# Seven-product block scheme in both feed-forward stages of a two-layer encoder kernel, with the Hyena filters moved between the output products

## The chip, the cores and the metric

The kernel runs on one core of one Trainium2 chip. The metric is the device time of one execution in microseconds (us). Engine names: PE is the matmul engine (TensorE), DVE VectorE, ACT ScalarE, POOL GpSimd, SP SyncE, which issues most DMAs. SBUF is the on-chip memory, PSUM the eight accumulator banks that PE writes.

## What is computed

768 tokens (512 of a prompt, 256 of a sample) of width 1024 pass two layers. Each layer is a half feed-forward step, a mixing part (RWKV-7 heads, neighbourhood attention, Hyena long convolution) and a second half feed-forward step. The reference, cut to what the change touches:

```python
def swiglu(x, w_in, w_out):
    gate, up = jnp.split(x @ w_in, 2, axis=-1)          # w_in 1024 x 5632, w_out 2816 x 1024
    return (jax.nn.silu(gate) * up) @ w_out

def encoder_layer(x, lp):
    x = x + 0.5 * swiglu(rms_norm(x, lp['norm_ffn1']), lp['ffn1_w_in'], lp['ffn1_w_out'])
    h = rms_norm(x, lp['norm_mix'])
    ...                                                  # mixing part, ends with x = x + mixed @ w_out
    return x + 0.5 * swiglu(rms_norm(x, lp['norm_ffn2']), lp['ffn2_w_in'], lp['ffn2_w_out'])

def hyena_filters(seq_len, lp):                          # 256 channels, two orders, two segments
    ...                                                  # z: 33 position features
    h = jnp.sin(freq * (z @ lp['hy_ff_w1'] + lp['hy_ff_b1']))
    h = jnp.sin(freq * (h @ lp['hy_ff_w2'] + lp['hy_ff_b2']))
    h = (h @ lp['hy_ff_w3']).reshape(seq_len, 2, HY_ORDER, C_DIM)
    h = h * jnp.exp(-t * jnp.abs(deltas))[:, None, None, :]
    ...                                                  # forward and flipped backward taps, joined to kern
    return kern / jnp.sum(jnp.abs(kern), axis=0, keepdims=True)   # its spectrum is used by the mixer
```

## The kernel before

**Data.** x lies transposed in SBUF, features on partitions: 8 tiles of 128 features x 768 tokens. Every main product is made of three matmuls (mm3, L898): each operand is split into a high part in fp32r and a low part, the rest, and high x high, high x low and low x high are added in PSUM. ACT makes the high part (a cast), DVE the low part (a subtraction). The token axis is cut into halves of 384 columns, so almost all matmuls have 384.

**Weights.** They come from memory in tiles of 1024 x 128 through wring, three buffers filled by SP in order of use (load_tile, L732). A buffer is refilled when DVE has made the low part of what it held (released, L719). The splits go to the rings wh and wl, 4 slots or 8 half slots.

**First feed-forward stage** (ffn, PE L987, ACT L1671, DVE L2209). 22 tiles of 128 gate features and as many of up features, in blocks of 6, 6, 5 and 5. For each tile j and token half PE makes gate and up: 2 x 8 x 3 = 48 matmuls, so 96 for a tile. ACT and DVE make the gated activation from them and split it. After a block the output part follows: 8 output tiles, two halves each, 3 matmuls for each of the block's tiles; DVE adds each result to x (add_out, L2146, who waits for PE there). Banks 0 to 3 belong to the input part, 4 to 7 to the output part. Behind the gate/up products stand the Hyena filter jobs, at the places named by FILTER_AT (a place is one token half of one tile): mlp (the two small layers), taps (the third layer, windowed by DVE, magnitudes taken by ACT, added up by POOL), sum (their total over partitions) and kern (the kernel's spectrum, by products with a table). They use banks 4 to 6.

**Second feed-forward stage** (ffn_pairs, PE L1050, ACT L1725, DVE L2315). Features are seen as 2 halves of 4 tiles, tokens as 2 halves, and [gate up] as 2 columns: a 2x2 block product made of seven products instead of eight. For a pair j of gate and up tile each product is 4 x 3 = 12 matmuls (product, L1036), 84 for the pair. A product i needs item i of the weights (a half tile of wring, or a sum that DVE makes in wsum at L2248, L2249 and L2257; split at L2267) and combination i of x (made once before the stage by pair_first and pair_second, L2373 and L2384, from x, gain and y1). Exits from PSUM: first_gate (L2276, L2277), second_up (L2284, L2286), second_gate (L2293, L2294), first_up, then gate_up twice and act_low1 twice; some products are held meanwhile by an ACT copy (hold, L1704). Blocks are 5, 5, 4, 4, 4. The ring has eight half slots: while pair j is multiplied, the items of pair j+1 are made (ahead), seven ahead. Output parts are as in the first stage.

**What sets the order.** Each engine runs its own program in the order written, and waits on semaphores. The combinations for the second stage are made while PE runs the last product of the mixing part (mix_out), whose tiles take 8 x 2 x 3 matmuls, in the order 0, 4, 1, 5, ... that completes pairs of tiles. The norm's sum of squares (add_squares, L2107) is joined to PE by norm (L904); its root (rstd) is not needed before the exits, since it scales columns.

## Time and profile before

| what | value |
|---|---|
| runs, device time | 3453.22, 3447.7, 3457.7 us; median 3453.22 |
| the profiled execution | 3456.03 us, of which the span of the engines 3454.2 |
| mean granted PE clock | 0.988 of full speed |
| PE, weight loads, DVE, ACT, POOL busy | 96%, 90%, 61%, 33%, 1% of the span |
| chain that ended last | PE 88%, DVE 8% |
| main matmuls with hh/hl (first stage and projections) | 3 x 2112, mean 340, 336 and 335 ns |
| main matmuls with the output activation | 3 x 1408, mean 335 ns |
| seven-product matmuls (L1033) | 3 x 1232, mean 336, 335 and 335 ns |

Matmuls overlap in the pipeline, so the duration of one is about twice the distance from one start to the next; costs are taken from distances. The order of stages in layer 0: first feed-forward stage from 28 to 617 us, projections and mixing to 1214, second feed-forward stage to 1730; layer 1 repeats this.

### The profile page before, as it was taken

To read this page: it belongs to the slowest core of one execution; us is meant where nothing else is said; L and a number is where in the kernel's file an instruction comes from. 1 tells how busy PE (TensorE), PEld (TensorE's weight loads), DVE (VectorE), ACT (ScalarE), POOL (GpSimd) and SP (SyncE) were. 2 spreads that over 40 slices of the span, in tenths; PEclk is the share of its full clock that TensorE was granted. 3 is DMA by queue.
4 is the path that set the end of the run, shared out by engine and by line. 5 is a ranking of instruction groups with operands and counts; after the bars stand their busy time and mean duration, and the time that the engine had idled before them with its cause. 6 is when DMAs were issued, how large, how long until landed. Compare 5 with 4: busy or idle time off the path is not lost.

```text
span 3454.2 us, 61563 instructions
## 1 busy us (share of the span) xinstructions
PE 3322.5 (96%) x26092; PEld 3125.4 (90%) x26092; DVE 2113.3 (61%) x3792; ACT 1153.1 (33%) x2015; POOL 50.4 (1%) x62
## 2 busy tenths in 40 slices
PE   7999999999998999999999999999999979999998
PEld 7999999888776899999999999998887768999997
DVE  5443444663878686666754534456548886776666
ACT  4221213221445353333431212132224544443333
POOL 0000000000000000000000000000000000000000
PEclk9999999999999999999999999999999999999999
DMA  3122121222033222222222121222310512222221
GB/s 136 61 78 69 61 74 56 104 96 85 4 115 137 68 62 73 72 68 68 69 77 80 63 84 48 73 88 78 106 59 5 197 54 80 65 69 72 71 68 67
DMA packets 80770, 264.36 MB, mean 77 GB/s; under 512 B 8994, under 2 KB 8994, under 8 KB 79216
## 3 DMA queue, kind: packets, MB, share of 16 engines
q1 hardware_dynamic: 76944, 248.08, 21.9%
q0 software_dynamic: 3552, 12.34, 1.1%
q8 instruction: 207, 3.39, 0.4%
q14 instruction: 67, 0.55, 0.1%
HBM read 230.50 MB, written 29.88 MB: 75 GB/s over the span
## 4 chain that ended last, share of the span: by engine, by line
PE 88%; DVE 8%; issue 2%; DMA 1%; ACT 1%; SPq 0%; DVEq 0%; ACTq 0%
PE ps L896 70%; PE ps L1033 18%; DMA gtab<-hyc 1%; DVE rstd L2107 0%; DVE uv L2735 0%; DVE sc L2785 0%; DMA bias<-bias 0%; DMA x<-xT 0%; PE ps L1489 0%; DVE M2X L2508 0%; ACT mh L2024 0%; DVE wl L2267 0%; DVE Mrk L2495 0%; DVE hout L2893 0%; DVE ktok L2496 0%
## 5 line engine op out<-in xcount | busy, mean ns | idle before, releaser
L896 PE MATMUL ps<-hh,wh 128*128 128x384 f32 (+2 forms) x2112 | 717.3, 340 | 11.5 <-DVE hl L2115 10.4
L896 PE MATMUL ps<-hl,wh 128*128 128x384 f32 (+2 forms) x2112 | 708.8, 336 | 0.0
L896 PE MATMUL ps<-hh,wl 128*128 128x384 f32 (+2 forms) x2112 | 708.4, 335 | 0.0
L896 PE MATMUL ps<-act_high,wh 128*128 128x384 f32 x1408 | 471.3, 335 | 1.7 <-DVE act_low L2313 1.7
L896 PE MATMUL ps<-act_high,wl 128*128 128x384 f32 x1408 | 470.4, 334 | 0.0
L896 PE MATMUL ps<-act_low,wh 128*128 128x384 f32 x1408 | 470.4, 334 | 0.0
L1624 ACT CAST wh<-wring 128x1024 fp32r<-128x1024 f32 (+3 forms) x300 | 261.7, 888 | 573.9 <-PE ps L896 541.6
L896 PEld LDWEIGHTS ps<-hh,wh 128*128 128x128 f32 x2112 | 398.8, 189 | 35.3 <-issue 16.0
L1033 PE MATMUL ps<-gh,wh 128*128 128x384 f32 x1232 | 414.1, 336 | 12.6 <-DVE gated L2284 4.3
L2146 DVE SCALAR_TENSOR_TENSOR x<-ps,x 128x384 f32<-128x384 f32 x320 | 177.4, 556 | 391.1 <-PE ps L896 390.9
L1033 PE MATMUL ps<-gh,wl 128*128 128x384 f32 x1232 | 412.9, 335 | 0.0
L1033 PE MATMUL ps<-gl,wh 128*128 128x384 f32 x1232 | 412.7, 335 | 0.0
L896 PEld LDWEIGHTS ps<-hl,wh 128*128 128x128 f32 x2112 | 399.1, 189 | 15.0 <-issue 0.3
L896 PEld LDWEIGHTS ps<-hh,wl 128*128 128x128 f32 x2112 | 398.7, 189 | 14.1
L2097 DVE TENSOR_TENSOR wl<-wring,wh 128x1024 fp32r<-128x1024 f32 (+3 forms) x300 | 304.2, 1027 | 67.6 <-ACT wh L1624 65.7
L896 PEld LDWEIGHTS ps<-act_high,wh 128*128 128x128 f32 x1408 | 264.3, 188 | 4.2 <-DVE act_low L2313 3.7
L896 PEld LDWEIGHTS ps<-act_low,wh 128*128 128x128 f32 x1408 | 264.3, 188 | 0.0
L896 PEld LDWEIGHTS ps<-act_high,wl 128*128 128x128 f32 x1408 | 264.3, 188 | 0.0
L1033 PEld LDWEIGHTS ps<-gh,wh 128*128 128x128 f32 x1232 | 232.4, 189 | 16.9 <-DVE gated L2284 5.0
L2221 DVE TENSOR_TENSOR silu<-ps,rstd 128x384 f32<-128x384 f32 x88 | 48.9, 556 | 323.3 <-PE ps L896 323.3
L1033 PEld LDWEIGHTS ps<-gl,wh 128*128 128x128 f32 x1232 | 232.4, 189 | 0.0
L1033 PEld LDWEIGHTS ps<-gh,wl 128*128 128x128 f32 x1232 | 232.1, 188 | 0.0
(305 smaller groups left out, 4642.1 us busy)
## 6 DMA issues: line engine op xcount, KB each, us to landing
wring<-wa SPq DMA_DIRECT2D x244, 512.0 KB, 3.5
wring<-wa SPq DMA_DIRECT2D x64, 320.0 KB, 2.8
wring<-wa SPq DMA_DIRECT2D x32, 384.0 KB, 3.1
bias<-bias SPq DMA_DIRECT2D x24, 512.0 KB, 8.3
wring<-wa SPq DMA_DIRECT2D x48, 256.0 KB, 2.5
conv_q_k<-stage SPq DMA_DIRECT2D x28, 384.0 KB, 2.6
kern_rows<-kst POOLq DMA_DIRECT2D x12, 512.0 KB, 3.3
outT<-x SPq DMA_DIRECT2D x2, 3072.0 KB, 10.3
```

Source lines behind the costliest of these rows:

```text
L896: return pe.matmul(out, lhsT, rhs, start=start, stop=stop)
L1033: m = pe.matmul(out, lhs[a], rhs[b], start=start and n == 0, stop=stop and n == 2, skip_group_check=onto)
L1624: sa.copy(wh[:, slot_of(t), 0:k, :], wring[:, t % RAWS, 0:k, :]).then_inc(s_whi, 1)
L2097: TT(wl[:, slot_of(t), 0:k, :], wring[:, t % RAWS, 0:k, :], wh[:, slot_of(t), 0:k, :].bitcast(F32), SU)\
L2146: STT(xs, bank(banks + v % 4, HALF), factor, xs, M, AD).then_inc(s_xup, 1)
L2221: TT(silu[:, u % 2, :], bank(2 * (u % 2), HALF), rstd[:, cols], M).then_inc(s_gate, 1)
```

## The change

Both feed-forward stages use ffn_pairs, and the ffn of three engines is gone. Six parts:

1. The first stage makes 84 matmuls for a pair in place of 96. Its combinations of x are made by start() in layer 0, and in layer 1 while PE runs the last output part of layer 0, whose tiles come in the order 0, 4, 1, 5, ... (pair_done with g = 2l + 2).
2. Blocks are 3, 3, 4, 4, 4, 4 in both stages.
3. The weight ring has 4 half slots (RING), and items, output tiles of the feed-forward part among them, are made three ahead (LEAD). The other half of the old ring's space holds filter buffers.
4. Filter jobs stand behind the output products of the first stage, at most to place 13 of the 16 of a block, and use banks 0 to 3.
5. They run in two halves of 128 channels: twice the jobs (24 of taps and kern in place of 12, 8 sums in place of 4), half the columns. hwt and dec hold one half at a time, and there is one table buffer.
6. x is loaded in pairs of tiles i and i + 4, and the kernels are stored by halves, in pieces of 128 columns.

The places of the filter jobs, block by block: block 0 has mlp at 0 and 4, taps at 9 and 10, sum 13; block 1 kern 0 and 4, taps 5 and 6, sum 9, kern 10; block 2 kern 0, taps 1, sum 4, kern 5, taps 6, sum 9, kern 10 (place 42 of the stage), taps 11 and 12 (places 43 and 44, the first of the second half); blocks 3 and 4 go on in the same way.

```diff
-FF_BLOCKS = [[(0, 6), (6, 6), (12, 5), (17, 5)], [(0, 5), (5, 5), (10, 4), (14, 4), (18, 4)]]
-FF_MOST = [max(n for _, n in b) for b in FF_BLOCKS]
-FF_OUTS = [2 * OUT_TILES * len(b) for b in FF_BLOCKS]
-FF_USES = [2 * FT + len(b) * OUT_TILES for b in FF_BLOCKS]
+FF_BLOCKS = [(0, 3), (3, 3), (6, 4), (10, 4), (14, 4), (18, 4)]
+FF_MOST = max(n for _, n in FF_BLOCKS)
+FF_OUTS = 2 * OUT_TILES * len(FF_BLOCKS)
+FF_USES = 2 * FT + len(FF_BLOCKS) * OUT_TILES
...
-UNITS = 7
-HALVES = 2 * SPLITS
+UNITS, RING, LEAD = 7, 4, 3
...
+FF_ITEMS = [t for b, (j0, nj) in enumerate(FF_BLOCKS)
+            for t in [("unit", j, i) for j in range(j0, j0 + nj) for i in range(UNITS)] + [("out", b, m) for m in range(OUT_TILES)]]
+ITEM_OF = {t: q for q, t in enumerate(FF_ITEMS)}
+ITEM_BASE = (2, 0)
...
-FILTER_AT = {2: ("mlp", 1), 5: ("mlp", 2), 7: ("taps", 0, 0, 0), 8: ("taps", 0, 0, 2), 9: ("sum", 0, 0),
-             13: ("kern", 0, 0), 14: ("kern", 0, 1), 15: ("taps", 1, 0, 0), 16: ("taps", 1, 0, 2), 18: ("sum", 1, 0),
-             20: ("kern", 1, 0), 21: ("kern", 1, 1), 25: ("taps", 0, 1, 4), 27: ("sum", 0, 1), 29: ("kern", 0, 2),
-             35: ("taps", 1, 1, 4), 37: ("sum", 1, 1), 39: ("kern", 1, 2)}
...
+CHH = C_DIM // 2
+TAP_GROUPS = [(h, o, s) for h in range(2) for s in range(2) for o in range(2)]
+KERN_ORDER = {(0, 0): (0, 1), (1, 0): (1, 0), (0, 1): (2,), (1, 1): (2,)}
...
+    jobs = [(0, ("mlp", 1)), (4, ("mlp", 2)), (4, None)]
+    for h, o, s in TAP_GROUPS:
+        jobs += [(1, ("taps", h, o, s, p)) for p in TAP_TILES[s][::2]] + [(3, ("sum", h, o, s))]
+        jobs += [(4 if n else 1, ("kern", h, o, a)) for n, a in enumerate(KERN_ORDER[o, s])]
+    out, at = {}, 0
+    for gap, job in jobs:
+        at += gap
+        if at % 16 > 13:
+            at = at // 16 * 16 + 16
...
+        def item_free(l, f, q):
+
+            if q >= RING:
+                return item_used(l, f, q - RING)
+            if f:
+                return s_fo, x_count(l, 2) + 2 * (4 + ring_place(f, q) // 2) + 2
...
+                for n, (h, o, s) in enumerate(TAP_GROUPS):
+                    add_magnitudes(l, n)
+                    p_last = TAP_TILES[s][-1]
+                    if o == 1 and (h, s) != (1, 1):
+                        pool.wait_ge(*fv.at(l, "win", h, o, p_last))
+                        load_decay(h + s, 1 - s)
+                    for a in KERN_ORDER[o, s]:
+                        pool.wait_ge(*fp.at(l, "kern", h, o, a))
+                        after = {(0, 0): 1, (1, 1): 0, (1, 0): 2, (1, 2): 0}.get((o, a))
+                        if after is not None and (h, o, a) != (1, 1, 2):
+                            load_table(after)
+                        if (h, o, a) == (0, 1, 2):
+                            pool.wait_ge(*fv.at(l, "skip", h, o, s))
+                            load_taps_weights(l, 1)
+                        pool.wait_ge(*fv.at(l, "scaled", h, o, a))
+                        kern_to = kern_d[l, o, a].rearrange("p (k c) -> p k c", c=C_DIM)[:, :, CHH * h:CHH * h + CHH]
+                        pool.dma_start(kern_to, kst[:, :, :]).then_inc(s_kst, 16)
...
+                            if f == 0:
+                                filters(l, v)
...
-                        ahead(j, 0)
+                            first_up(J - 1, 3 - ba)
+                            gate_up(J - 1, 0)
+                        items_to(l, f, q + LEAD)
                         if j > j0:
-                            act_low1(l, j - 1, 1)
-                            act_low1(l, j - 1, 0)
-                        ahead(j, 1)
-                        ahead(j, 2)
-                        ahead(j, 3)
+                            act_low1(J - 1, j - 1 - j0, 1)
+                            act_low1(J - 1, j - 1 - j0, 0)
+                        for i in (1, 2, 3):
+                            items_to(l, f, q + i + LEAD)
                         if j == 0:
                             norm()
-                        first_gate(l, j)
-                        ahead(j, 4)
-                        second_up(l, j)
-                        ahead(j, 5)
-                        second_gate(l, j)
-                        ahead(j, 6)
-                        gate_up(l, j, 1)
-                    first_up(l, j)
-                    gate_up(l, j, 0)
-                    act_low1(l, j, 1)
-                    act_low1(l, j, 0)
+                        first_gate(J, ba)
+                        items_to(l, f, q + 4 + LEAD)
+                        second_up(J, ba)
+                        items_to(l, f, q + 5 + LEAD)
+                        second_gate(J, ba)
+                        items_to(l, f, q + 6 + LEAD)
+                        gate_up(J, 1)
...
+            def start():
+
+                ve.wait_ge(s_par, 16)
+                for i in range(KH):
+                    ve.wait_ge(s_x[i], 16)
+                    first_sum(0, i)
+                    first_low(0, i)
+                items_to(0, 0, 0)
+                for i in range(KH):
+                    second_sum(0, i)
+                for i in range(KH):
+                    sum_low(0, i, "T1", "T2")
+                items_to(0, 0, 1)
+                for i in range(KH):
+                    third_sum(0, i)
+                for i in range(KH):
+                    fourth_sum(0, i)
+                for i in range(KH):
+                    sum_low(0, i, "T2", "T4")
+                items_to(0, 0, 2)
+                for i in range(KH):
+                    second_low(0, i)
+                items_to(0, 0, 3)
+                for i in range(KH):
+                    sum_low(0, i, "T3")
+                items_to(0, 0, 5)
+                for m in range(KT):
+                    add_squares(m)
+                for i in range(KH):
+                    sum_low(0, i, "T4")
+                items_to(0, 0, 6)
```

What the code does is clearest in the engines' own order. **DVE, middle of a block of the second stage.** Before, from the last exits of one pair to the first of the next (wl is a low part, wsum a weight sum, held a saved product):

```order
L2306 TENSOR_TENSOR gated_89<-silu_88,gated_89 128x384 [waits silu1_done,partial_out_of_bank]
L2248 TENSOR_TENSOR wsum<-wring 128x512 [waits unit_split_ready,w_tile_loaded2,w_tile_loaded1]
L2249 TENSOR_TENSOR wsum<-wring 128x512
L2267 TENSOR_TENSOR wl<-wring,wh 128x512 [waits unit_high_ready]
L2313 TENSOR_TENSOR act_low_67<-gated_89,act_high_66 128x384 [waits act1_high_ready] x2
L2267 TENSOR_TENSOR wl<-wsum,wh 128x512 [waits unit_high_ready]
L2257 TENSOR_TENSOR wsum<-wsum,wring 128x512 [waits unit_split_ready,weight_sums_made]
L2267 TENSOR_TENSOR wl<-wsum,wh 128x512 [waits unit_high_ready]
L2257 TENSOR_TENSOR wsum<-wring,wsum 128x512 [waits unit_split_ready,weight_sums_made]
L2267 TENSOR_TENSOR wl<-wring,wh 128x512 [waits unit_high_ready]
L2276 TENSOR_TENSOR ps<-ps,held_85 128x384 [waits partial_held,unit_product_ready]
L2277 TENSOR_TENSOR silu_88<-ps,rstd 128x384 [waits vector_step]
```

After, from the same exit of a pair (L2308 is first_gate's addition, L2268, L2269 and L2277 are the weight sums, L2288 the low parts):

```order
L2308 TENSOR_TENSOR ps<-ps,held_85 128x384 [waits partial_held,unit_product_ready]
L2309 TENSOR_TENSOR silu_88<-ps,rstd 128x384 [waits vector_step]
L2268 TENSOR_TENSOR wsum<-wring 128x512 [waits unit_split_ready,w_tile_loaded2,w_tile_loaded1]
L2269 TENSOR_TENSOR wsum<-wring 128x512
L2288 TENSOR_TENSOR wl<-wring,wh 128x512 [waits unit_high_ready]
L2315 TENSOR_TENSOR gated_89<-ps,held_86 128x384 [waits partial_held,unit_product_ready]
L2317 TENSOR_TENSOR gated_89<-gated_89,rstd 128x384 [waits partial_out_of_bank]
L2288 TENSOR_TENSOR wl<-wsum,wh 128x512 [waits unit_high_ready]
L2277 TENSOR_TENSOR wsum<-wsum,wring 128x512 [waits unit_split_ready,weight_sums_made]
L2323 TENSOR_TENSOR ps<-ps,held_87 128x384 [waits partial_held,unit_product_ready]
L2324 TENSOR_TENSOR silu_88<-ps,rstd 128x384 [waits vector_step]
L2288 TENSOR_TENSOR wl<-wsum,wh 128x512 [waits unit_high_ready]
```

The four weight sums and the first three low parts of the next pair have moved from before first_gate to between the exits behind it.

**POOL, filter loads and stores of the first stage.** Before, around the change of segment (one change of dec and table, hwt stays):

```order
L853 TENSOR_TENSOR acc<-acc,taps 128x512 [waits magnitudes_added,filter_activated] x3
L840 DMA table_103<-hyc 128x2x512 [waits magnitudes_added]
L863 DMA kern_rows<-kst 128x1024 [waits filter_vector] x2
L834 DMA dec<-hyc 128x512 [waits filter_vector]
L840 DMA table_102<-hyc 128x2x256 [waits filter_products]
L850 COPY acc<-taps 128x512 [waits filter_vector,filter_activated]
```

After, around the change of channel half (places 38 to 43):

```order
L932 COPY acc<-taps 128x256 [waits filter_vector,filter_activated]
L935 TENSOR_TENSOR acc<-acc,taps 128x256 [waits magnitudes_added,filter_activated]
L913 DMA dec<-hyc 128x4x128 [waits filter_vector]
L922 DMA table<-hyc 128x2x512 [waits filter_products]
L917 DMA hwt<-hyw 65x512 [waits filter_vector]
L963 DMA kern_rows<-kst 512x1x128 [waits filter_vector]
L932 COPY acc<-taps 128x256 [waits filter_vector,filter_activated]
```

The load of hwt for the second half is new, and stands behind a load of the table that waits for the kern job's products.

**PE, the same place.** Before, a taps job between products of the input part (hh, hl are the normalised x):

```order
L896 MATMUL ps<-hl,wh 128x384
L896 MATMUL ps<-hh,wl 128x384
L896 MATMUL ps<-hwt,h_95 128x256 x4
L896 MATMUL ps<-hh,wh 128x384
L896 MATMUL ps<-hl,wh 128x384
```

After, the end of the kern job at place 42 and the taps job at 43; between its last row and the hwt row stand the 12 matmuls of one output product, of which the last are shown:

```order
L980 MATMUL ps<-se,table 128x128
L980 MATMUL ps<-h_98,cst 128x128
L980 MATMUL ps<-so,table 128x128
L980 MATMUL ps<-se,table 128x128
L980 MATMUL ps<-so,table 128x128
...
L980 MATMUL ps<-act_low_67,wh 128x384
L980 MATMUL ps<-act_high_66,wl 128x384
L980 MATMUL ps<-hwt,h_98 128x128 x4
L980 MATMUL ps<-act_high_66,wh 128x384
```

The filter rows have half the columns, and their neighbours are output products.

## Rows read from the trace of the kernel before

**Rows 1.** The page: busy time of each engine, and the chain by engine.
```profile
PE 3322.5 (96%) x26092; PEld 3125.4 (90%) x26092; DVE 2113.3 (61%) x3792; ACT 1153.1 (33%) x2015; POOL 50.4 (1%) x62
...
PE 88%; DVE 8%; issue 2%; DMA 1%; ACT 1%; SPq 0%; DVEq 0%; ACTq 0%
```

**Rows 2.** Timeline, first stage of layer 0: start, duration (us), engine, line, instruction.
```profile
28.10 1.09 PE L896 MATMUL ps<-hh,wh 128*128 128x384 f32 x1
...
616.32 0.56 DVE L2146 SCALAR_TENSOR_TENSOR x<-ps,x 128x384 f32<-128x384 f32 x1 [1.25 <-PE ps L896]
```

**Rows 3.** Timeline of PE: filter jobs, and 128-column matmuls of the attention.
```profile
95.00 2.00 PE L896 MATMUL ps<-hwt,h 64*128 64x256 f32 x8
96.93 0.44 PE L896 MATMUL ps<-hh,wh 128*128 128x384 f32 x1
...
199.93 1.02 PE L896 MATMUL ps<-se,table 128*128 128x256 f32 x4
...
204.02 0.53 PE L896 MATMUL ps<-hh,wh 128*128 128x384 f32 x1
...
1027.90 1.09 PE L1489 MATMUL ps<-cst,sc 128*128 128x128 f32 x8
```

**Rows 4.** Timeline of DVE, second stage of layer 0, within one block.
```profile
1481.19 0.57 DVE L2293 TENSOR_TENSOR ps<-ps,held 128x384 f32<-128x384 f32 x1 [0.33 <-PE ps L1033]
1481.79 0.56 DVE L2294 TENSOR_TENSOR silu<-ps,rstd 128x384 f32<-128x384 f32 x1
1482.26 0.68 DVE L2267 TENSOR_TENSOR wl<-wring,wh 128x512 fp32r<-128x512 f32 x1
...
1484.47 0.69 DVE L2248 TENSOR_TENSOR wsum<-wring 128x512 f32<-128x512 f32 x1
1485.08 0.69 DVE L2249 TENSOR_TENSOR wsum<-wring 128x512 f32<-128x512 f32 x1
...
1487.22 0.68 DVE L2267 TENSOR_TENSOR wl<-wsum,wh 128x512 fp32r<-128x512 f32 x1
1488.01 0.69 DVE L2257 TENSOR_TENSOR wsum<-wsum,wring 128x512 f32<-128x512 f32 x1
...
1495.75 0.57 DVE L2293 TENSOR_TENSOR ps<-ps,held 128x384 f32<-128x384 f32 x1 [0.33 <-PE ps L1033]
```

**Rows 5.** SyncE's weight load there, and the DMA list's weight loads.
```profile
1478.81 0.33 SPq L736 DMA_DIRECT2D wring<-wa  x1
...
wring<-wa SPq DMA_DIRECT2D x244, 512.0 KB, 3.5
```

**Rows 6.** Timeline of DVE, last pair of a block of four.
```profile
1510.31 0.57 DVE L2293 TENSOR_TENSOR ps<-ps,held 128x384 f32<-128x384 f32 x1 [0.93 <-PE ps L1033]
...
1515.05 0.56 DVE L2146 SCALAR_TENSOR_TENSOR x<-ps,x 128x384 f32<-128x384 f32 x1 [0.23 <-PE ps L896]
```

**Rows 7.** Start of layer 0: the chain's load of x, and timeline.
```profile
3.56 10.77 DMA x<-xT
...
19.56 6.27 DVE L2107 TENSOR_TENSOR rstd<-rstd,sqb 128x768 f32<-128x768 f32 x6 [0.91 <-ACT sqb L1632]
...
25.98 2.90 PE L896 MATMUL ps<-rstd,cst 128*128 128x384 f32 x4 [7.80 <-DVE rstd L2107]
...
30.00 0.85 ACT L1605 ACTIVATE rstd<-rstd 128x768 f32<-128x768 f32 x1
```

**Rows 8.** Timeline: mixing part to second stage (layer 0), and layer 0 to layer 1.
```profile
1206.60 0.61 DVE L2392 SCALAR_TENSOR_TENSOR tsum<-x,par,tsum 128x384 f32<-128x384 f32 x1
...
1211.92 0.69 DVE L2267 TENSOR_TENSOR wl<-wsum,wh 128x512 fp32r<-128x512 f32 x1
...
1734.76 1.53 PE L896 MATMUL ps<-rstd,cst 128*128 128x384 f32 x4 [0.16 <-DVE rstd L2107]
```

**Rows 9.** GpSimd's filter loads: timeline, and the DMA list (us to landing last).
```profile
36.11 0.73 POOL L840 DMA_DIRECT2D table<-hyc  x1
...
hwt<-hyw POOLq DMA_DIRECT2D x2, 260.0 KB, 5.3
```

1108 lines of the change are left out of this document (538 added, 570 removed).

## Prediction

> **What bounds the kernel now.** I read the page's busy shares first: TensorE (PE) is busy 96% of the span, and the chain of work that ended last is PE for 88% [rows 1]. So in the feed-forward stages, which the change touches, a matmul taken away is worth its full price, unless something else is then late. Next I read the edges of the first feed-forward stage of layer 0 in the timeline: its steady part runs from 28.10 to the last output tile's addition at 616.32, 588.2 us [rows 2]. The second stage already uses the seven-product scheme, and its vector rows give the price of a matmul: the waits of L2293 for product 5 come at 1481.19 and 1495.75, one pair of feature tiles apart, so 84 matmuls of 384 columns take 14.56 us, 0.1733 us each, or 2.08 us for a product of 12 [rows 4]. Of the 588.2 us, 3144 such matmuls (24 of the 3168 were done before 28.10) are 544.9; the other 43.3 are filter matmuls. Eighteen filter jobs account for that (below), so PE hardly waits in this stage, and every microsecond of wait that the change brings is new.
>
> **What the change removes.** The first stage's input part goes from 96 to 84 matmuls for each of 22 pairs in two layers: 528 x 0.1733 = **-91.5 us**. The output matmuls are the same in number.
>
> **Filters on PE.** Before, a taps job (4 instructions of 256 columns, 8 rows in the trace) takes 1.93 us (95.00 to 96.93), and a kernel job of four tiles 4.09 (199.93 to 204.02), of which the one-row bias term is about 0.65 [rows 3]; coming back to the main stream costs 0.2 more each. In channel halves there are twice as many of each with 128 columns. The nearest row of 128 columns and 128x128 weights in f32 is 1.09 us for 8, at most 0.136 each [rows 3]. So a taps job is 8 x 0.13 + 0.25 = 1.3, a kernel job 16 x 0.13 + 0.65 + 0.2 = 2.9 (1.9 for the short segment). A layer: taps 12 x 1.3 against 6 x 2.13 (+2.8), kernels 8 x 2.9 + 4 x 1.9 against 4 x 4.3 + 2 x 2.55 (+8.5), sums +1.2. That is **+25 us** for two layers. Ends: +5 if half the columns cost half, +75 if a row of 128 columns costs what one of 256 does (164 more rows a layer at 0.23). I take the value near the 128-column row.
>
> **Start of layer 0.** Before, PE multiplies as normalised chunks arrive. Now product 0 needs the first combination of all four chunk pairs, and VectorE (DVE) makes five combinations and five low parts for each before the first pair is through. The last part of x lands at 14.33 [rows 7]. From there DVE's order is: to 16.1 the last sum and low part; weight sums and the first low part to 17.9; then four second sums 2.1, lows 1.9, item 1 with its sum 1.4, third and fourth sums 4.0, lows 1.9, item 2 1.4, the double-width lows 3.7, item 3 0.6, lows 1.8, items 4 and 5 1.2, which is 37.9; the seven additions of squares 8 (6.27 for six of them [rows 7]) to 45.9. The norm's product and root took from 25.98 to 30.85, and so end at 50.8. Then first gate 1.1, item 7 with two sums 1.8, bank exit 0.6, and product 6 at half clock 3: pair 0 ends at 57.3, as if the stage had begun at 42.7. Before it began, reckoned so, at 28.10 - 4.2 + 1 = 24.9. **+17.8 us**, most of it DVE work in series; ends 12 and 24.
>
> **Layer 0 to layer 1.** Before, this passage costs PE about 1.7 us (its norm at 1734.76 follows the last output product within 4.3 us, in which 24 matmuls ran [rows 8]). Now x must be combined while the last block's output tiles run, 4.16 us each. An odd tile's work on DVE is 5.32 us (1206.60 to 1211.92 [rows 8]), an even one's about 1.9 (two instructions of 384 and the squares' addition); with two additions (0.95) and the lows that is 10.6 us for two tiles that PE makes in 8.3. Laid out from the first output product (0), DVE ends its last tile at 49.3, while PE ends at 34.0; product 2 starts at 50, the norm at 54.2, product 6 near 61, pair 0 ends at 63.3 against 47.9 without a wait. 15.4 - 1.7 = **+13.7 us**; ends 8 and 20.
>
> **Block starts.** When the input part of a block ends, the last pair's activation is late: product 5 ends at 1510.31, so 6 ends at 1512.39, and the first output product of 12 matmuls (2.08) ends at 1515.05, 0.58 late [rows 6]. With three tiles it needs that activation after 6 matmuls, not 9, so 1.1 late. Blocks of five or six tiles hide it. Before: three blocks of four a layer, 1.7 us. After, in both stages: four of three and eight of four, 9.0. **+14.5 us** for two layers. Block (3,3) starts at an odd pair, whose banks overlap the output's: with filter work on DVE behind it, 1.5 a layer in the first stage, **+3**.
>
> **Filter waits.** In the first stage's output part a product lasts 1.56 or 2.08 us, where a job before had 8.3 us to itself. Taps at place 10 of block 0 and their sum at 13 leave 4.7 us for DVE, ScalarE and GpSimd, with DVE already some 3 us behind: about 1.3 us. The weights of the second channel half (hwt) are loaded after the last kernel job of the first half (place 42) and used at place 43, one product later. GpSimd first issues the table (0.73), then hwt, which lands after 5.3 [rows 9]: 6.1 - 2.08 = 4.0 us of wait. With 0.8 for small ones, 6.1 a layer, **+12**; ends 4 and 50. Here a page of the Trainium skill would have it shorter: "DMA: Bandwidth & Descriptors", section "Anatomy of one DMA", gives about 2 us and the bytes over 436 GB/s for such a load from GpSimd. By that 130 KB take 2.3 us, an estimate from the page, and the wait is 1.0 in place of 4.0, 6 us less in all; the trace's 5.3 us for twice the bytes speaks against it, and it enters no number here.
>
> **The shorter ring.** Items are now made three ahead, not seven. In a pair DVE has about 11.8 us of work in 14.56 (11 instructions of 384 and 11 of 512 by the distances below), but it sits differently: the four weight sums fall between the bank exits. I laid one pair out from first gate (0), with 0.60 from start to start for a 512-element instruction and for a dependent one of 384, 0.47 for an independent one and 0.79 from a low part to the sum behind it [rows 4]: weight sums at 1.07, low 7 at 2.3, second up 2.9, low 8 and sum to 5.3, second gate, low 9 and sum to 7.8, gate and up to 9.5, low 10, low 11 ending 11.7. That last one releases the next up tile; SyncE issues such a load at once (the one at 1478.81 came with the end of a low part), and it lands 3.5 later [rows 5], at 15.2. The next weight sums are due at 15.6. So this loop has 0.4 us to spare, and held 0 (9.8, due 10.4) 0.6. I take **0** for steady pairs. Cover gone, a loop of 15.1 us would cost 0.5 for each of the 64 pairs that don't open a block: +32. A gain is excluded, since PE has no idle time there. A gain there is, though, behind the mixing stage: ScalarE no longer makes the next pair's items ahead of the norm, so the root comes 1.3 and product 6 of the first pair about 2 us earlier, an estimate from the order of its work, **-4** for two layers.
>
> **Sum.** -91.5 + 25 + 17.8 + 13.7 + 14.5 + 3 + 12 - 4 = -9.5 us. The profiled execution took 3456.0, 2.8 more than the median of the runs, 3453.2; a difference carries over, so the forecast is **3444 us** on the median's scale. A measurement of this kernel tells 0.3% (10.4 us) from no change, so this is the edge between faster and same.
>
> **Rivals.** (1) The saving mostly stays: filter rows of 128 columns at half price, waits at starts and loads half of mine. Filters +10, block starts 9, filter waits 6, start and passage 25: about 3425. For it speaks that DVE's laid-out chains add pessimistic ends; against it the row of 128 columns. Chance 0.2. (2) The ring binds: the weight loop (low 11, load, weight sums) is longer than 14.56 us. It decides as soon as the landing takes over 3.9 us or DVE lags by 0.4; priced at 0.5 us a pair it gives 3476, slower. For it: only 0.4 us to spare over a load of 3.5; against: other items have more slack. 0.17. (3) Output blocks become DVE's: with filters among them DVE has up to 5 us for a tile that PE makes in 3.1 to 4.2, and PE waits at filter jobs and at additions; 2.5 us for each of 12 blocks more gives about 3473. For it: DVE's 2.2 us for a taps job, two in a row; against: four banks let PE run four products ahead. 0.15. (4) The forecast, with its own range of 3432 to 3458: 0.48.
>
> **How the numbers follow.** Of (4) half lies below 3442.8: faster 0.2 + 0.23; same 0.25 and a little of (1) or (3): 0.27; slower (2), (3): 0.30. The range from 3422 to 3475 leaves out the tails of (1) and (2).
>
> **What would show it.** In the profile after: PE matmuls fewer by 528; first output product of a block 0.6 or 1.1 late; PE idle before the ninth taps row group (L980) near 4 us, released by GpSimd's load; pair 0 of layer 0 ending near 57; two waits of L2308 14.56 us apart in both stages (15 or more: rival 2); PE idle at L980 or at output products released by DVE's additions beyond 1 us a block: rival 3. If 128-column filter rows are spaced 0.2 us, the filter term fails; if DVE's passage between layers ends before 45, that one does.

## The result, and the profile of the changed kernel

| | median of 20 runs | profiled execution | its span |
|---|---|---|---|
| before | 3451.9 us | 3456.0 us | 3454.2 us |
| changed | 3458.0 us | 3455.2 us | 3453.4 us |

The ratio of changed to before is 1.0016, 95% interval 1.0010 to 1.0023: 6.1 us slower, which is within 0.3% and inside the stated range, but on the other side of the forecast (9.5 us faster). The two profiled executions differ by 0.8 us the other way. Half of the story is thus in the terms of the sum, and half in how the two executions stand to their medians. Both are taken apart below.

The page of the changed kernel, its first lines, its chain and its first group of instructions (of before, [rows 1] answer):

```profile
span 3453.4 us, 63597 instructions
PE 3263.6 (95%) x25876; PEld 3063.6 (89%) x25876; DVE 2488.0 (72%) x4660; ACT 1316.1 (38%) x2491; POOL 74.9 (2%) x112
...
PE 81%; DVE 13%; issue 3%; ACT 2%; DMA 1%; SPq 0%; DVEq 0%; POOL 0%; ACTq 0%
...
L1064 PE MATMUL ps<-gh,wh 128*128 128x384 f32 x2464 | 833.5, 338 | 63.6 <-DVE wl L2288 25.9
```

TensorE is busy 59 us less than before, and the span is the same: the work that went has become idle time, and VectorE's share of the chain that ended last is 13%. The wait list of TensorE says where (engine, line, what it waited for: us in total, times, longest). Read it by line: L1064 is the seven-product matmul, so its waits are those of stage openings and odd block starts, and two short ones in the middle of blocks, shown below.

```profile
PE ps L1064 <- DVE wl L2288: 25.9, 4, 19.2
...
PE ps L1064 <- DVE gated L2315: 13.6, 6, 5.5
PE ps L980 <- DVE act_low L2340: 11.1, 24, 0.8
...
PE ps L1064 <- issue: 7.4, 3, 6.0
...
PE ps L980 <- DMA hwt<-hyw: 6.3, 2, 3.2
...
PE ps L1064 <- DVE x L2196: 4.5, 2, 2.2
```

By stage, from the end of one stage's last addition to x to the end of the next one's (in the timeline of VectorE; us):

| | layer 0: first | mixing | second | layer 1: first | mixing | second |
|---|---|---|---|---|---|---|
| before | 616.9 | 599.3 | 514.9 | 592.8 | 598.3 | 514.9 |
| changed | 614.9 | 597.0 | 523.7 | 581.0 | 598.9 | 520.8 |

The first stage of layer 0 gives back nearly all that it saves; that of layer 1 gains 11.8, but the second stage ahead of it loses 8.8, in good part the passage between the layers; the last one loses 5.8. Outside mixing that is 0.9 us more in all. Mixing is the same code in both, and 1.7 us shorter in this trace.

Five places carry the argument. **The load of the second channel half's weights**, from TensorE's timeline (start, duration, instruction, idle time before it and what ended it), and the granted clock in three stretches around it:

```profile
304.75 1.46 PE L980 MATMUL ps<-hwt,h 64*128 64x128 f32 x8 [3.22 <-DMA hwt<-hyw]
306.13 0.69 PE L980 MATMUL ps<-act_high,wh 128*128 128x384 f32 x1
306.62 0.52 PE L980 MATMUL ps<-act_low,wh 128*128 128x384 f32 x1
306.94 0.52 PE L980 MATMUL ps<-act_high,wl 128*128 128x384 f32 x1
```
```profile
core 0: us, PE busy (x) PEld busy (x) DVE busy (x) ACT busy (x) POOL busy (x), PEclk, DMA share, GB/s
296.00:301.50 5.50, 5.50 (x34) 4.96 (x32) 5.07 (x10) 0.50 (x2) 1.27 (x2) 1.00 0.19 41
305.50:308.80 3.30, 3.30 (x12) 3.08 (x11) 2.12 (x8) 1.34 (x3) 0.86 (x2) 0.50 0.02 5
308.90:312.00 3.10, 3.10 (x20) 2.73 (x19) 2.96 (x7) 0.22 (x1) 0.16 (x1) 1.00 0.00 0
```

The wait is 3.22 us. Behind it the clock is 0.50 (1.2 GHz), and the matmuls stand 0.320 apart instead of 0.173: nine of them cost 1.4 us that no wait list shows. In layer 1 the wait at the same place is 3.08 us, and the slow clock takes in the filter rows too. **A block start**, here of the first block of three: the late matmul of the first output product starts at 90.93, 1.15 us behind its predecessor instead of 0.17, and the next one 0.28 behind it; 1.08 late in all.

```profile
89.78 0.34 PE L980 MATMUL ps<-act_high,wl 128*128 128x384 f32 x1
90.93 0.44 PE L980 MATMUL ps<-act_high,wh 128*128 128x384 f32 x1 [0.81 <-DVE act_low L2340]
91.21 0.34 PE L980 MATMUL ps<-act_low,wh 128*128 128x384 f32 x1
```

**The start of layer 0**: VectorE adds squares until 47.2, the norm's sum begins then, and the last product of pair 0 at 55.85. **The passage** from layer 0 to layer 1: three long waits of TensorE, and VectorE's last addition of squares at 1743.35. The first output product of that block began at 1694.35.

```profile
40.99 6.27 DVE L2158 TENSOR_TENSOR rstd<-rstd,sqb 128x768 f32<-128x768 f32 x6 [0.92 <-ACT sqb L1669]
47.41 2.90 PE L980 MATMUL ps<-rstd,cst 128*128 128x384 f32 x4 [4.28 <-DVE rstd L2158]
55.85 0.69 PE L1064 MATMUL ps<-gh,wh 128*128 128x384 f32 x1 [5.54 <-DVE gated L2315]
```
```profile
1734.82 0.66 PE L1064 MATMUL ps<-gh,wh 128*128 128x384 f32 x1 [6.00 <-issue]
1745.01 0.41 PE L1064 MATMUL ps<-gh,wh 128*128 128x384 f32 x1 [3.05 <-ACT held L1737]
1758.88 0.44 PE L1064 MATMUL ps<-gh,wh 128*128 128x384 f32 x1 [2.43 <-DVE gated L2315]
```
```profile
1743.35 0.95 DVE L2158 TENSOR_TENSOR rstd<-rstd,sqb 128x768 f32<-128x768 f32 x1
```

And **the steady pairs**: first gate's waits in VectorE's timeline are 14.56 us apart, as in [rows 4] (first two rows). Two pairs are not steady. In the one shown, VectorE's weight sum waits for a weight load that took 4.89 us from issue to landing (median 3.5), and TensorE then waits for VectorE; the other is at 3278.1 (load 4.84 us, wait 0.37).

```profile
231.63 0.57 DVE L2308 TENSOR_TENSOR ps<-ps,held 128x384 f32<-128x384 f32 x1 [0.35 <-PE ps L1064]
246.19 0.57 DVE L2308 TENSOR_TENSOR ps<-ps,held 128x384 f32<-128x384 f32 x1 [0.35 <-PE ps L1064]
...
459.87 0.69 DVE L2268 TENSOR_TENSOR wsum<-wring 128x512 f32<-128x512 f32 x1 [0.97 <-DMA wring<-wa]
...
462.29 0.44 PE L1064 MATMUL ps<-gh,wh 128*128 128x384 f32 x1 [0.42 <-DVE gated L2315]
```

### The profile page after: what moved, and what is told of

Read it like the earlier page. It is cut to its first block, busy times and chain, and to the rows that moved or that the text cites. A ratio compares the mean times of both kernels' runs of the same rounds, so it can differ in the third digit from the quotient of the medians.

```text
span 3453.4 us, 63597 instructions
## 1 busy us (share of the span) xinstructions
PE 3263.6 (95%) x25876; PEld 3063.6 (89%) x25876; DVE 2488.0 (72%) x4660; ACT 1316.1 (38%) x2491; POOL 74.9 (2%) x112
## 4 chain that ended last, share of the span: by engine, by line
PE 81%; DVE 13%; issue 3%; ACT 2%; DMA 1%; SPq 0%; DVEq 0%; POOL 0%; ACTq 0%
PE ps L980 47%; PE ps L1064 34%; DVE uv L2809 1%; DVE wl L2288 1%; DVE gated L2334 1%; DMA wring<-wa 1%; DVE x L2196 0%; DVE rstd L2158 0%; DVE ps L2323 0%; DVE silu L2324 0%; PE ps L1528 0%; DVE gl L2427 0%; DVE gated L2329 0%; DVE wl L2149 0%; DVE act_low L2340 0%
## 5 line engine op out<-in xcount | busy, mean ns | idle before, releaser
L1064 PE MATMUL ps<-gh,wh 128*128 128x384 f32 x2464 | 833.5, 338 | 63.6 <-DVE wl L2288 25.9
L1064 PE MATMUL ps<-gl,wh 128*128 128x384 f32 x2464 | 829.6, 337 | 0.0
L1064 PE MATMUL ps<-gh,wl 128*128 128x384 f32 x2464 | 829.4, 337 | 0.0
L1064 PEld LDWEIGHTS ps<-gh,wh 128*128 128x128 f32 x2464 | 467.5, 190 | 73.0 <-DVE wl L2288 21.8
L980 PE MATMUL ps<-act_high,wh 128*128 128x384 f32 x1408 | 482.0, 342 | 11.3 <-DVE act_low L2340 11.1
L1064 PEld LDWEIGHTS ps<-gl,wh 128*128 128x128 f32 x2464 | 467.4, 190 | 0.4
L1064 PEld LDWEIGHTS ps<-gh,wl 128*128 128x128 f32 x2464 | 467.3, 190 | 0.0
L2288 DVE TENSOR_TENSOR wl<-wsum,wh 128x512 fp32r<-128x512 f32 x352 | 240.9, 690 | 78.5 <-ACT wh L1717 77.7
L2288 DVE TENSOR_TENSOR wl<-wring,wh 128x512 fp32r<-128x512 f32 x264 | 182.3, 690 | 124.9 <-ACT wh L1717 121.5
L980 PE MATMUL ps<-hh,wh 128*128 128x256 f32 (+1 forms) x704 | 238.6, 339 | 1.0 <-DVE raw L2499 1.0
L980 PE MATMUL ps<-hl,wh 128*128 128x256 f32 (+1 forms) x704 | 237.1, 337 | 0.0
L980 PE MATMUL ps<-hh,wl 128*128 128x256 f32 (+1 forms) x704 | 236.7, 336 | 0.0
L2149 DVE TENSOR_TENSOR wl<-wring,wh 128x512 fp32r<-128x512 f32 (+2 forms) x260 | 208.2, 801 | 25.2 <-ACT wh L1661 22.5
```

The source lines that it names most:

```text
L980: return pe.matmul(out, lhsT, rhs, start=start, stop=stop)
L1064: m = pe.matmul(out, lhs[a], rhs[b], start=start and n == 0, stop=stop and n == 2, skip_group_check=onto)
L2149: TT(tile_part(wl, t), wring[:, t % RAWS, 0:tile_k(t), :], tile_part(wh, t).bitcast(F32), SU).then_inc(s_w, 1)
L2288: TT(ring_part(wl, f, q, KH), unit_raw(l, f, j, i), ring_part(wh, f, q, KH).bitcast(F32), SU).then_inc(s_ulo, 1)
```

## The experiments

Every kernel ran beside the one before on the same chip; ratios are to it. On this scale the changed kernel is 1.0016, and 0.001 is 3.5 us. Where two kernels are compared with each other, the difference of their ratios is uncertain by some 4 us (5 where few runs were made), so the traces are asked as well.

**What do the filters cost, before and after?** Two kernels without any filter work (every filter call, its loads and its waits taken out; the later read of the kernels is pointed at other data).

```
-                            filters(l, 2 * j + hf_, b)
...
-                                sp.dma_start(kern[o][a][:, :, :, :].rearrange("p k t c -> p (k t c)"), kern_d[l, o, a])\
+                                sp.dma_start(kern[o][a][:, :, :, :].rearrange("p k t c -> p (k t c)"), wa[l, 3 * o + a])\
```

> The kernel before without its filter work (the small network, taps, sums and kernel jobs of the first feed-forward stage are left out on every engine, and Hyena reads other numbers in their place). Both theories agree here, since it is the yardstick: in the trace of before the filter jobs and the returns from them hold TensorE about 39 us a layer and nothing waits for them, so about 78 us less than the 3451.9 of before, 3374.

> The changed kernel with the same filter work left out. Theory A (filters cost by their waits too): beside 49 us a layer of filter rows and returns, each layer loses 7 to 8.5 us at waits inside filter jobs with the slow matmuls behind them and about 3.9 us at the start of the second block, so about 122 us less than 3458.0, 3336, and 38 less than the kernel before without filters. Theory B (only the rows cost, the waits sit there for another reason, such as the weight ring or late additions, and stay): about 99 us less, 3359, and 15 less than the kernel before without filters.

Measured: before 3367.8 (0.9754, 0.9740 to 0.9769), changed 3335.1 (0.9660, 0.9646 to 0.9674). The filters cost 84 us before (by the medians, 3451.9 - 3367.8) and 123 after, and without them the change is worth 32.7 us. Theory A holds, and B falls: the waits inside the filter jobs go with them. Without filters the start of the second block still waits, 0.70 us instead of 2.25, so 1.55 of that one was the filters'.

**One load.** The tap weights of the second half are loaded as soon as their last reader is done:

```
                     for a in KERN_ORDER[o, s]:
+                        if (h, o, a) == (0, 1, 2):
+                            pool.wait_ge(*fv.at(l, "skip", h, o, s))
+                            load_taps_weights(l, 1)
                         pool.wait_ge(*fp.at(l, "kern", h, o, a))
...
-                        if (h, o, a) == (0, 1, 2):
-                            pool.wait_ge(*fv.at(l, "skip", h, o, s))
-                            load_taps_weights(l, 1)
```

> The changed kernel with the load of the second channel half's tap weights issued as soon as their last reader is done, before the kernel job instead of behind it and a table load. Theory A (a wait of 3.2 us and the half-clock matmuls behind it cost about 4.8 us a layer): both go, 3448.5. Theory B (VectorE is behind there anyway, and TensorE waits for the taps row instead): within 1 us of 3458.0.

Measured 3446.4 (0.9982, 0.9974 to 0.9991), 11.7 under the changed kernel, give or take 4, for 6.3 us of waits in the list. The job runs without a wait, and the clock is 1.00 there:

```profile
300.00:310.00 10.00, 10.00 (x60) 9.26 (x59) 8.12 (x21) 2.13 (x5) 2.93 (x5) 1.00 0.26 80
```

A holds. The place itself gives a closer figure: from VectorE's 41st addition to x in the stage to its 48th, which enclose the job, the changed kernel takes 24.0 us in layer 0 and 25.1 in layer 1, this one 19.5 in both. That is 10.0 us for waits of 6.3. The price of a wait was about 1.6 times its length.

**Does the low clock cost something of its own?** Idle matmuls on constants, into a bank that nobody reads, fill the longest waits:

```
+            def warm(n, b):
+                for _ in range(n):
+                    mm(bank(b, HALF), cs("ones"), cst[:, COFF["masks"]:COFF["masks"] + HALF])
...
+                    if job[1:] == (1, 0, 0, 0):
+                        warm(4, 0)
                     pe.wait_ge(s_hz, 64 * l + 48 + 16 * h)
```

> The changed kernel with idle matmuls (on constants, into a bank that nobody reads) put where TensorE waits longest: four ahead of the wait for the second channel half's weights, three ahead of the second block, and in the passage between the layers seven ahead of pair 0, three ahead of its third and three ahead of its last product. Theory A (behind each such wait TensorE runs at half clock for a while, and that is a cost beside the wait): the granted clock stays up in these places, 1.4 to 2 us less at each of four places in the stages and up to 6 in the passage, 3446 to 3452. Theory B (the clock costs nothing that the waits do not cost already, since VectorE sets the end of these stretches): 3457 to 3461.

Measured 3448.7 (0.9996, 0.9987 to 1.0005), 7 us under the changed kernel, give or take 4, though nothing that TensorE waits for comes sooner. The granted clock of the passage, first of the changed kernel, then of this one:

```profile
1734.00:1762.30 28.30, 21.53 (x88) 20.09 (x89) 21.36 (x41) 15.19 (x25) 2.39 (x4) 0.80 0.19 56
```
```profile
1734.00:1762.00 28.00, 23.99 (x116) 20.24 (x117) 22.17 (x43) 15.35 (x26) 2.39 (x4) 1.00 0.20 57
```

The first addition of the next block comes 97.2 us after the first of this one in the changed kernel, 94.6 here. The place of the late weights is 1.5 and 2.6 us shorter (22.5 and 22.4 for 24.0 and 25.1). A holds, at the lower end of what it gave.

**Where the blocks of three stand.**

```
-FF_BLOCKS = [(0, 3), (3, 3), (6, 4), (10, 4), (14, 4), (18, 4)]
+FF_BLOCKS = [(0, 4), (4, 4), (8, 4), (12, 3), (15, 3), (18, 4)]
```

> The changed kernel with the two blocks of three moved from the front to the fourth and fifth place of each stage (4, 4, 4, 3, 3, 4 tiles); the number of blocks and matmuls is the same. Theory A (the waits around the first block, 1.2 for taps, 1.3 for a sum and 2.2 at the odd start of the second block with slow matmuls behind it, are there because the first filters meet products of 1.56 us instead of 2.08): about 5 us less a layer in the first stage, 3448 to 3450. Theory B (the waits belong to the filters' own chain and to any odd block start, wherever it stands): within 2 us of 3458.0.

Measured 3449.1 (0.9997, 0.9988 to 1.0006), 6.6 less; in its trace the two first stages are 5.3 and 4.5 us shorter. The waits for taps and for the sum in the first block are gone, and the odd start, now behind the fourth block, waits 0.70 us:

```profile
437.92 0.41 PE L1064 MATMUL ps<-gh,wh 128*128 128x384 f32 x1 [0.70 <-issue]
```

A holds: the filters' first, long chain met output products that were too short for it.

**Blocks or ring in the second stage?** The kernel before, with only the blocks of its second stage changed:

```
-FF_BLOCKS = [[(0, 6), (6, 6), (12, 5), (17, 5)], [(0, 5), (5, 5), (10, 4), (14, 4), (18, 4)]]
+FF_BLOCKS = [[(0, 6), (6, 6), (12, 5), (17, 5)], [(0, 3), (3, 3), (6, 4), (10, 4), (14, 4), (18, 4)]]
```

> The kernel before with its second feed-forward stage alone cut into the six blocks of the changed kernel (3, 3, 4, 4, 4, 4 for 5, 5, 4, 4, 4), its ring and look-ahead as they were. Theory A (block starts cost 0.8 us with three tiles and 0.3 with four, by TensorE's waits in the changed kernel, and the odd start 0.7): the second stages lose 2 us each, 3456. Theory B (the prediction's price of block starts, 1.1 and 0.6 us): 3457.5. Theory C (what the second stages lose comes from the shorter ring): 3452.

Measured 3465.9 (1.0045, 1.0031 to 1.0059), slower than all three theories gave. The second stages take 520.5 and 520.7 us in its trace, 5.7 more than before, with the old ring. So C falls. That the changed kernel takes the same 520.8 in layer 1 is in part chance: there the odd start is cheaper and the opening dearer. A and B priced too few things: beside the six starts, the odd start waits 2.71 us under the old ring (0.70 under the new one), and slow matmuls follow it. That makes 11.3 us for both stages, inside the interval (10.7 to 20.4).

```profile
1266.94 0.44 PE L896 MATMUL ps<-act_high,wh 128*128 128x384 f32 x1 [0.81 <-DVE act_low L2313]
1293.87 0.41 PE L1033 MATMUL ps<-gh,wh 128*128 128x384 f32 x1 [2.71 <-issue]
```

**Squares on GpSimd.** VectorE's additions of squares at the start and in the passage are made by GpSimd:

```
+                    pool.tensor_tensor(rstd[:, :], sqb[:, 0, :] if m == 1 else rstd[:, :], sqb[:, m % 2, :], ALU.add)
```

> The changed kernel with the additions of squares at the start of layer 0 and in the passage from layer 0 to layer 1 made by GpSimd instead of VectorE (in the start ScalarE also makes the squares earlier). Theory A (both stretches are VectorE's work in series, 8 and 7 us of which are these additions): pair 0 of layer 0 ends near 54 instead of 59.8, the passage is 6 to 8 us shorter, 3444 to 3446. Theory B (VectorE is not what ends last there, but the norm's chain, and GpSimd's additions of 768 columns take 2.1 us or more each and slow VectorE beside them): no gain, 3457 to 3464.

Measured 3466.3 (1.0040, 1.0027 to 1.0053), 8 us worse than the changed kernel, outside both. The timelines of GpSimd and of VectorE side by side show why:

```profile
23.79 2.03 POOL L945 TENSOR_TENSOR rstd<-rstd,sqb 128x768 f32<-128x768 f32 x1 [1.93 <-ACT sqb L1685]
```
```profile
24.08 2.29 DVE L2308 TENSOR_TENSOR wl<-wsum,wh 128x512 fp32r<-128x512 f32 x1
26.47 0.69 DVE L2297 TENSOR_TENSOR wsum<-wsum,wring 128x512 f32<-128x512 f32 x1
```

A low part that takes 0.69 us takes 2.29 when GpSimd's addition has begun ahead of it, and ends 0.55 after that does. VectorE loses 1.6 us, to be spared an addition of 0.95. All seven additions at the start meet a VectorE instruction that reads two operands in SBUF, and each such instruction takes 2.15 to 2.58 us, where the same ones take 0.55 to 1.01 alone. The Trainium skill, "SBUF — State Buffer", section "SBUF: two separate sides", states this: an operation of VectorE with two inputs in SBUF and one of GpSimd that reads SBUF exclude each other for the whole instruction. The trace agrees. The run says nothing for or against VectorE's work as the limit; for that the work had to go to an engine that doesn't block it.

**Squares on TensorE**, which is idle at the start: matmuls with ones, between the first products.

```
+                    for f in range(2):
+                        m = mm(bank(6 + f, HALF), cs("ones"), sqb[:, m_ % 2, f * HALF:(f + 1) * HALF], m_ == 0, m_ == KT - 1)
...
-                for m in range(KT):
-                    add_squares(m)
```

> The changed kernel with the sum of squares at the start of layer 0 made on TensorE, which is idle there: each tile's squares are multiplied with ones and accumulate in two banks, between the first products, in place of VectorE's seven additions; ScalarE makes the squares earlier. Theory A (VectorE's work in series sets the start): product 6 begins near 47 instead of 55.9 and pair 0 ends near 49 instead of 59.8, 3447 to 3449. Theory B (the products, slowed by half clock and by 12 to 20 us of matmuls for the squares, set the end instead): pair 0 ends at 57 or later, 3455 to 3461.

Measured 3440.4 (0.9972, 0.9961 to 0.9984), 15 less, for additions that lasted 8 us. The last product of pair 0 begins at 47.06:

```profile
47.06 0.44 PE L1078 MATMUL ps<-gh,wh 128*128 128x384 f32 x1 [1.38 <-DVE gated L2342]
```

A holds. It is 8.8 us earlier than in the changed kernel, at full clock, and the pair ends near 49.3 instead of 59.8; the rest of the span's 14.7 us lies in the mixing stages, which are 2.2 and 3.5 us shorter in this trace, though the edit doesn't touch them. The first stage of layer 0, where the edit is, is 9.5 us shorter: that much is shown to be its own.

**Squares left out of the passage** (8 of 768 columns are added):

```
-                add_squares(p)
+                add_squares(p, 8 if g == 2 else T)
```

> The changed kernel with VectorE's seven additions of squares in the passage between the layers cut to 8 columns of 768 (so most of the norm's sum is left out there). Theory A (in the passage VectorE's work in series sets the end): 7 x 0.87 us come off it, the last product of pair 0 begins near 58 us after the first output product of the block instead of 64.5, and the time is 6 to 9 us lower, 3449 to 3452. Theory B (the chain of output products, norm and root sets it, and the additions hide beside TensorE's output tiles): within 2 us of 3458.0.

Measured 3453.3 (1.0010, 1.0001 to 1.0018), 2 us less by the ratios and 5 by the medians, between the theories and too little to decide by the time alone. The last addition to x comes 34.2 us after the first instead of 37.5, and the next block's first output 4.3 us earlier. So the squares are 4.3 of the passage's 18 us. VectorE's other work still makes it late: it ends its last tile 45.6 us after the first output product, nearly 12 behind TensorE's outputs, and TensorE waits 3.09 and 2.27 us where it waited 6.00 and 3.05. The wait of 2.43 for `gated` behind the norm stays as it was.

**What lies behind the last tile.** The first product of pair 1 goes ahead of the last one of pair 0, which has to wait for the root and a bank exit, in all four stages:

```
+                        if j == 0:
...
+                            product(l, f, 1, 0)
                         pe.wait_ge(s_exit, 4 * J + 2)
                         product(l, f, j, 6)
```

> The changed kernel with the first product of pair 1 moved ahead of the last product of pair 0 in all four stages (its weights split ahead of the norm), so that TensorE has work while VectorE empties the bank after the root. Theory A (the price of each stage's opening that the prediction did not see is this wait, 2.4 us, and the slow matmuls behind it, 1.7 us, at three stages, and 5.5 us of wait at the start of layer 0): the waits shrink to under 0.5 us at three stages, 3 to 4 us each, 2 us at the start, 3444 to 3448. Theory B (VectorE, with items and bank exits one after another behind the root, sets the end there, and TensorE waits for the next low parts instead): 3456 to 3460.

Measured 3441.9 (0.9969, 0.9957 to 0.9981), 16 less, give or take 5. The wait for `gated` behind the norm is gone in the passage and at the second stages; at the start of layer 0, 2.3 us are left of 5.5, now for a low part. The next block's first addition in the passage comes after 93.1 us instead of 97.2; the last stage takes 515.0 us, as it did before the change. Up to each stage's first addition to x the four openings are 2.0, 2.4, 4.2 and 5.4 us shorter, 14.0 together. The first row is the start of layer 0; in the passage the other two waits stay, and so does the one of 6.00 ahead of them:

```profile
52.84 0.69 PE L1064 MATMUL ps<-gh,wh 128*128 128x384 f32 x1 [2.32 <-DVE wl L2295]
...
1737.90 0.45 PE L1064 MATMUL ps<-gh,wh 128*128 128x384 f32 x1 [0.97 <-DVE gl L2435]
1741.75 0.66 PE L1064 MATMUL ps<-gh,wh 128*128 128x384 f32 x1 [3.05 <-ACT held L1744]
```

A holds at three openings, and gave too little in all: VectorE is not what ends last there once TensorE has something else to do. At the start of layer 0 the wait that is left is the one that B named. The kernel before has this wait too, 2.15 and 2.18 us at its two second stages, so a part of the 16 us is no cost of the change.

**Together.** The early load, the block order and the squares on TensorE; these with idle matmuls in the passage; these with the exchanged products.

> Three edits at once on the changed kernel: the early load of the second half's weights, the blocks of three in fourth and fifth place, and the squares at the start of layer 0 on TensorE. Theory A (they cure separate waits, and their gains of 11.7, 7 and 15 us add up): 3424 to 3427. Theory B (a cured wait comes back at the next late unit, VectorE above all, so that only the largest two count): 3432 to 3438.

> The three edits and, in the passage between the layers alone, the idle matmuls (seven, three and three) that keep TensorE's clock up. Theory A (half clock behind the waits costs about 3 us in the passage beside them): 3420 to 3424, 3 to 4 us under the kernel with three edits. Theory B (the passage is VectorE's, and TensorE's clock costs nothing in it): the same as the kernel with three edits.

> The kernel with three edits (early load, blocks of three in fourth and fifth place, squares on TensorE) and this exchange of two products as the fourth. Theory A: 9 to 14 us under the kernel with three edits, 3408 to 3413. Theory B: the same as the kernel with three edits, 3421.

Measured: 3421.5 (0.9914, 0.9901 to 0.9928); 3420.8 (0.9912, 0.9899 to 0.9926); 3409.5 (0.9877, 0.9864 to 0.9890). The three cures add up: 35 us together, 33.5 one by one. Idle matmuls bring nothing more that can be told (0.7 us, as B had it): in that trace pair 0's last product comes 1.9 us later after the block's first addition than in the kernel with the three edits (61.7 against 59.9), so what the clock gave, the fillers took. Real work in the gap brings 12 us more. This last kernel beats both the one before and the changed one: it is 1.23% under the one before. Its page:

```profile
span 3408.0 us, 63646 instructions
PE 3254.6 (95%) x25904; PEld 3054.3 (90%) x25904; DVE 2481.4 (73%) x4653; ACT 1315.3 (39%) x2491; POOL 75.4 (2%) x112
```

## Why the prediction was wrong

The terms, for two layers. Found values are from TensorE's starts in the two traces: the time from one matmul to the next, less 0.1733 for each of the main stream, sorted by what stands on both sides.

| term | forecast | found |
|---|---|---|
| 528 matmuls | -91.5 | -91.5 |
| filter rows and the return from them | +25 | +14 |
| start of layer 0 | +17.8 | +20.3 |
| layer 0 to layer 1 | +13.7 | +18.4 |
| block starts, the odd start, late weight loads | +17.5 | +18.6 |
| filter waits | +12 | +19.4 |
| mixing to second stage | -4 | +1.6 |
| sum | -9.5 | +0.8 |

Outside mixing the traces differ by +0.9, so the sum closes; single terms are read to 1 us or so. What the filters add at the odd starts, 3.1 us, stands with the filter waits. Mixing adds -1.7, and the traces differ by -0.8. The sum was thus 10.3 us too low: openings and passage were 12.8 too low, filter waits 7.4, block starts 1.1, and filter rows 11 too high. That the time stayed inside the range owes much to this last error, which stood against the others: that is luck.

**Right.** A matmul taken away was worth its price: 11616 matmuls in the input and output products of the four stages stand where 12144 stood, and TensorE's rows of the main stream are spaced as before. The shorter ring costs next to nothing in steady pairs (14.56 apart; two late weight loads, 0.8 us of waits in the whole trace; before, VectorE waits for loads up to 1.32 us in such places, and TensorE never for that). Block starts came as laid out, 1.08 late with three tiles for the 1.1 of the text, 0.56 with four for 0.58. The weights of the second half were waited for, 3.2 us where 4.0 stood: the load took 4.2 us from GpSimd's issue to its landing, not the 5.3 of the row for twice the bytes. The estimate from the Trainium skill ("DMA: Bandwidth & Descriptors", "Anatomy of one DMA"), 2.3 us and a wait of 1.0, was further off. In the passage VectorE ended its last tile 50 us after the first output product (49.3 in the text), TensorE its outputs after 34.5 (34.0).

**Filter rows: mis-sized, in favour.** With the two or three matmuls behind them that come late, and without waits and the half clock, all jobs take 41.7 us a layer before and 48.7 after: 7.0 more, where the text had 12.5. The price of the jobs before was right (35.0 without sums and the small network, 35.1 in the text). Of the halved ones the taps jobs were right too (1.36 us each, 1.3 in the text); the kernel jobs were priced too high, at 2.9 and 1.9 for 2.40 and 1.51, and the sums at 1.2 a layer more for 0.4.

**The first failed step: what a wait costs (7.4 us too low).** Each wait was priced at its length. The filter waits themselves are 10.0 us in the two first stages, and 3.1 at the odd starts behind filters; but 6.3 us more are matmuls at half clock behind them. The run with the early load shows it (10.0 us at the place for waits of 6.3), and that with idle matmuls (7 us with every cause of a wait left in). The filters as a whole rose by 38.8 us, 122.9 against 84.1, where the text had 37, or 40 with its odd starts: too much for rows, too little for waits, and right in total only by luck.

**The second failed step, and the larger: openings (12.8 us too low).** The chain behind the last square (sum, root, first gate, bank exit, product 6) was laid out too short. In the start the root ends at 52.3 (50.8 in the text) and the pair 7.5 behind it (6.5). In the passage the norm's sum starts 56.5 after the first output product (54.2), the root ends at 59.9, product 6 starts at 64.5, at half clock, and the pair ends at 68.0 instead of 63.3: 11.5 behind the sum, where the text had 9.1. The same chain stands at both second stages, where the text had a gain of 2 each, since ScalarE is free sooner: it is, but the product waits 2.43 us for `gated` all the same, where it waited 2.15 and 2.18 before. Up to the first product of pair 1 the opening is 0.6 us shorter than before in layer 0 and 2.3 longer in layer 1: there the half clock follows the wait, in layer 0 it does not; before, it did in both. Without filters the change was worth 32.7 us, 14 less than the text's terms without filters (46.5). Of this 12.8 are the openings (2.5, 4.7 and 5.6). The exchange of two products takes away the wait behind the norm alone and wins 14 us in the four openings of its trace, so that wait and the half clock behind it are a large part of what the openings cost. How much of the 12.8 is that wait alone, and how much VectorE's late combinations in front of it, no run separates.

**The scale.** The forecast carried the profiled execution's distance from its median, 2.8 us then, over to the changed kernel. Over 20 runs it was 4.2 above for the one before, and 2.8 below for the changed one. So 7 of the 15.6 us between forecast and measurement are this step. It is no term of the change, and the record shows what it goes with: the granted clock. In the 20 executions of the changed kernel the mean granted clock is 0.980 to 0.984, and 0.001 less goes with 1.3 us more; the profiled one is among the fastest, at 0.984. The profiled execution of the kernel before had 0.988, where the median of those beside the experiments is 0.990 or 0.991. The same wait of 2.43 us is followed by the half clock in one execution and not in the next: the opening of a second stage takes 54.6 us up to the first addition in layer 0 and 57.7 in layer 1, with the same work. The layer's mixing, the same code in all traces, took 594.2 to 600.0 us in layer 0; 599.3 in the profiled execution of before, 597.0 in that of the changed kernel. How the 7 us divide among such places stays open.

**The rivals.** (1) was near on filter rows (+14 for its +10) and wrong on every opening; its terms as written add up to 3408, not to the 3425 of the text. (2) did not decide: the loop held in steady pairs, but its mechanism is there, as foreseen for a landing over 3.9 us, in two pairs of this trace. (3), output blocks that become VectorE's, happened in the first block alone, where taps (1.2), in layer 0 the sum (1.3), and the second block's start (2.2) wait; moving the blocks of three cured it for 6.6 us.

## What to carry to other kernels

Price a wait of TensorE with the matmuls behind it: here two waits of 3.2 and 3.1 us cost 10.0. Where a short chain over several engines (norm, root, bank exit) ends in one matmul product, put an independent product ahead of it before trying to shorten the chain; that was worth as much as taking the squares from VectorE, and real work won 12 us where idle matmuls won none that could be told. Before a profiled execution's distance from its median is carried over to another kernel, compare the granted clocks of both. When a scheme turns a spread input into one that needs all of it, lay out the opening of every stage, not only of the one that is changed.

## What the runs showed of the hardware

- TensorE's granted clock went to 0.50 (1.2 GHz) behind each of these waits: at 305.5 behind 3.22 us without work, in the passage at the waits of 6.0, 3.05 and 2.43. Matmuls of 384 columns then start 0.320 us apart, 0.173 at full clock. It doesn't follow every time: behind the wait of 2.43 at the second stage it stayed at 1.00 in layer 0 (at 1231.5) and fell to 0.50 in layer 1 (at 2936.6). With the waits filled by idle matmuls it stayed at 1.00 through the passage.
- GpSimd and VectorE exclude each other when both read two operands in SBUF: 2.29 us for 0.69, and so at all seven additions at the start of that run.
- Matmuls with half the columns (128 for 256) at 64x128 weights: the 8 rows of a taps job took 1.14 us up to the next instruction, where the 8 rows with 256 columns took 1.93 [rows 3].
- Weight loads of 512 KB land after 3.5 us in the median; single ones took 4.84 and 4.89 us, and with items made three ahead that is enough to stop TensorE for 0.4 us.
